# Summing the two halves of a gate weight in two TensorE products instead of in VectorE's addition, in every second batch of a gate table

## The reference, cut to what matters

```
s = einsum('bthpd,phnd->bthpn', q, sub_keys)          # 8 heads, 2 sides, 128 keys
sv, si = top_k(s, 16)                                 # per side
cand = sv[..., 0, :, None] + sv[..., 1, None, :]      # 16 x 16 candidates a head
cv, ci = top_k(cand, 16)
e1, e2 = the two key numbers of each of the 16        # expert = e1 * 128 + e2
gate = softmax(cv)
act = gelu(einsum('td,ted->te', hh, u_tab[ii]))
out = einsum('te,ted->td', gg * act, v_tab[ii])
x = x + out
```

## Time and profile before

| | us |
|---|---|
| median of three runs | 2497.33 |
| lowest and highest | 2496.42 and 2497.46 |
| profiled execution, its own time | 2494.71 |
| its span (first to last instruction) | 2492.9 |
| TensorE busy with products | 2435.0 (98%) |
| TensorE weight loads | 2278.8 (91%) |
| VectorE busy | 1666.5 (67%) |
| ScalarE busy | 1307.7 (52%) |
| GpSimd busy | 1126.6 (45%) |

### The profile page before, as it was taken

One profiled execution on the slowest core, in us unless ns is written; L12 is line 12 of the kernel. 1 busy time (PEld: TensorE's weight loads), 2 busy tenths in 40 slices (PEclk: granted clock), 3 DMA queues, 4 the chain that ended last, 5 costly groups with the idle time before them and its releaser, 6 DMA issues.

```text
span 2492.9 us, 46157 instructions
## 1 busy us (share of the span) xinstructions
PE 2435.0 (98%) x17096; PEld 2278.8 (91%) x17096; DVE 1666.5 (67%) x3053; ACT 1307.7 (52%) x2000; POOL 1126.6 (45%) x452
## 2 busy tenths in 40 slices
PE   9999999999999999999999999999999999999998
PEld 7999998999999998888799999999999999988886
DVE  7455713799997555777673666237999975567775
ACT  5565545555555444555555655555555554445554
POOL 4865776798674000000067767667976730000000
PEclk9999999999999999999999999999999999999999
DMA  6543554455667666777654335444557676667773
GB/s 225 169 135 113 168 186 135 148 175 174 247 238 253 223 206 223 243 243 244 207 180 157 133 127 169 163 150 152 184 181 248 239 257 205 216 227 236 237 243 132
DMA packets 186555, 485.59 MB, mean 195 GB/s; under 512 B 14400, under 2 KB 80960, under 8 KB 181824
## 3 DMA queue, kind: packets, MB, share of 16 engines
q1 hardware_dynamic: 179808, 442.74, 53.5%
q10 hardware_dynamic: 6624, 41.16, 4.8%
HBM read 449.24 MB, written 34.60 MB: 194 GB/s over the span
## 4 chain that ended last, share of the span: by engine, by line
PE 86%; DVE 6%; ACT 3%; POOL 2%; DMA 1%; issue 1%; SPq 0%; DVEq 0%; ACTq 0%; POOLq 0%
PE banks L800 28%; PE banks L464 17%; PE banks L466 16%; PE banks L465 16%; PE banks L776 2%; POOL w_lo L394 2%; PE banks L621 1%; ACT w_hi L832 1%; DVE arena L1596 1%; PE banks L720 1%; PE banks L704 1%; PE banks L685 1%; DVE arena L1439 1%; DMA o_f<-gates_dram 0%; DVE arena L1529 0%
## 5 line engine op out<-in xcount | busy, mean ns | idle before, releaser
L394 POOL TENSOR_TENSOR w_lo<-ring,w_hi 128x1024 fp32r<-128x1024 f32 x448 | 1126.4, 2526 | 899.2 <-ACT w_hi L832 898.7
L832 ACT ACTIVATE w_hi<-ring 128x1024 fp32r<-128x1024 f32 x776 | 816.9, 1056 | 406.0 <-PE banks L800 331.4
L464 PE MATMUL banks<-h_r,w_hi 128*128 128x256 f32 x3216 | 915.9, 285 | 2.7 <-DVE h_r L1364 1.8
L466 PE MATMUL banks<-h_r,w_lo 128*128 128x256 f32 x3216 | 911.2, 283 | 0.0
L465 PE MATMUL banks<-h_r,w_hi 128*128 128x256 f32 x3216 | 911.2, 283 | 0.0
L464 PEld LDWEIGHTS banks<-h_r,w_hi 128*128 128x128 f32 x3216 | 617.8, 192 | 7.9 <-issue 2.6
L465 PEld LDWEIGHTS banks<-h_r,w_hi 128*128 128x128 f32 x3216 | 617.9, 192 | 3.0 <-issue 0.5
L466 PEld LDWEIGHTS banks<-h_r,w_lo 128*128 128x128 f32 x3216 | 617.8, 192 | 0.0
L800 PE MATMUL banks<-w_hi,o_r 128*128 128x512 f32 x2048 | 559.2, 390 | 1.2 <-DVE o_r L1796 1.2
L800 PEld LDWEIGHTS banks<-w_hi,o_r 128*128 128x128 f32 x2048 | 380.3, 188 | 77.4 <-DVE o_r L1796 1.6
L1764 DVE TENSOR_TENSOR w_lo<-ring,w_hi 128x1024 fp32r<-128x1024 f32 x320 | 389.6, 1218 | 10.0 <-ACT w_hi L832 10.0
(11 more groups left out here) (268 smaller groups left out, 2609.9 us busy)
## 6 DMA issues: line engine op xcount, KB each, us to landing
ring<-in_stream SPq DMA_DIRECT2D x776, 512.0 KB, 3.3
gates_dram<-o_f ACTq DMA_DIRECT2D x32, 1024.0 KB, 5.5
o_f<-gates_dram SPq DMA_DIRECT2D x32, 1024.0 KB, 7.0
arena<-in_mem ACTq DMA_DIRECT2D x2, 1024.0 KB, 12.2
arena<-in_keys ACTq DMA_DIRECT2D x2, 1024.0 KB, 4.7
arena<-in_c_decay ACTq DMA_DIRECT2D x2, 768.0 KB, 5.3
x<-in_x SPq DMA_DIRECT2D x4, 256.0 KB, 5.8
out_dram<-arena SPq DMA_DIRECT2D x4, 256.0 KB, 2.3
```

What stands on the lines that cost most here:

```text
L394: pool.tensor_tensor(w_lo[:, s, :], ring[:, s, :], w_hi[:, s, :], ALU.subtract).then_inc(sem(f"low{s}"), 1)
L464: pe.matmul(out, lhs[0], rhs[0], start=first, stop=False)
L466: return pe.matmul(out, lhs[1], rhs[0], start=False, stop=last)
L832: act.activation(w_hi[:, s, :], ring[:, s, :], ACT.Copy).then_inc(sem(f"high{s}"), 1)
```

## The change

In batches of odd parity the four products of 256 columns become eight of 128 columns: for each token the high half and then the low half of `one2`, with the same `one1` as the stationary operand, into the same 128 columns of PSUM. The second of the two accumulates onto the first. ScalarE's copy (L1180) is unchanged and reads the first 128 columns of each token, which now hold the sum. VectorE's `spread_out` in these batches no longer adds: after the same wait for `table_high` it copies one column of PSUM to a scratch column and raises `spread_free`. Even batches are as before.

```diff
                     for t in range(BATCH):
-                        m = pe.matmul(table_out(parity)[:, t, :, :], one1[:, parity, t, :], one2[:, parity, t, :, :],
-                                      start=True, stop=True)
+                        if parity:
+                            for u in range(2):
+                                m = pe.matmul(table_out(parity)[:, t, 0, :], one1[:, parity, t, :], one2[:, parity, t, u, :],
+                                              start=(u == 0), stop=(u == 1))
+                        else:
+                            m = pe.matmul(table_out(parity)[:, t, :, :], one1[:, parity, t, :], one2[:, parity, t, :, :],
+                                          start=True, stop=True)
                     m.then_inc(sem("spread"), 1)
...
                     dve.wait_ge(sem("table_high"), l * BATCHES + i * (BATCHES // MIXED) + j + 1)
+                    if parity:
+                        dve.tensor_copy(mx[:, 0:1], bank[:, 0, 0:1]).then_inc(sem("spread_free"), 1)
+                        return
```

## The result

The changed kernel takes 2526.7 us (median of 4 runs, 2525.86 to 2529.03) against 2497.07 us for the kernel before on the same chip (4 runs, 2496.42 to 2497.46). The ratio is 1.012, 95% interval 1.0104 to 1.0136. The forecast was 2525.5 us, 28 us slower; it is 29.6 us slower.

A forecast was written before the change was run, and what follows sets the result against it. The prediction took TensorE to bound the woven stage: 2494.71 us profiled plus 28.2 for narrow products is 2522.9, plus 2.6 for the median gives 2525.5 us; own range 2518 to 2532, 8-in-10 range 2518 to 2590.

The forecast's parts named there:

- TensorE bounds the stage, VectorE is close behind: Woven stage: TensorE's own work sets the 3.36 us between batches; VectorE waits for it 17 times, 8.7 us in all.
- rival 3: Woven stage: VectorE was the hidden bound, so lightening it gives about 2470 us plus the products' cost; chance next to nothing.
- VectorE's edit is worth nothing: Odd batches, woven stage: VectorE gets some 26 to 37 us lighter, priced at zero because TensorE's work covers it.
- The load sets the pace of a narrow product: Odd batches: eight products at 0.115 us each, 0.44 us more a batch, 28.2 us in all; chance 0.52.
- The first and second rival: Odd batches: the first has narrow products at float32 rate, 2576 to 2595 us, chance 0.30; the second is rival 2.
- rival 2: Odd batches: weight loads partly or wholly hidden under the narrow products, 2495 to 2518 us; chance 0.15.
- The end of the stage moves with TensorE: Woven stage's end: gelu, two DMAs and TensorE's 0.61 us wait shift along, idle time stays, down stage does not move.
- The sum: Whole kernel: profiled 2494.71 us plus 28.2 makes 2522.9; plus 2.6 for the median of runs, 2525.5 us.

The follow-up runs named there:

- The early write: Changed kernel, but ScalarE issues the write of a half's last chunk of gates ahead of that step's gelu, not behind it: 2522.89 us, ratio 1.011.

## Why the prediction was right, step by step

**TensorE bounds the stage, VectorE is close behind.** Right. The run with VectorE's part alone moved nothing, and rival 3 had its test there. The view that told it beforehand was the table of waits and not the busy shares, in which both engines looked full.

**VectorE's edit is worth nothing.** Right, with 64 x (0.678 - 0.151) = 34 us taken from it (its busy time fell by 30.5), inside the 26 to 37 that were worked out.

**The load sets the pace of a narrow product.** Right, and the one step on which everything hung. The gap of 0.11 us between the first and the second load after idle time was the evidence; 0.115 us was taken, 0.112 measured. An odd batch costs 3.773 - 3.353 = 0.420 us more by the medians of the starts, where 0.44 was forecast, so 26.9 us in place of 28.2. The difference is the pace alone, 8 x 0.003 = 0.024 us a batch. The first product of an odd batch does give way to the second after 0.061 us, as its load is hidden under the 256-column product ahead of it, but the same time comes back at the end: the up product at L464 starts at 709.85 and L465 0.17 us later, since a load of 128 columns no longer fits under the last narrow product. From 709.00 to 710.02 makes 1.02 us, which is 8 x 0.112 + 0.12. The first and second rival fell with the same number, and the runs with 64 moving and 64 stationary columns showed that it is the load and not the width of the product. The sustained figure of 81 ns at 128 columns, from the Trainium skill, "TensorE: Matmul & The Clock Gate", section "Back-to-back issue gap", held for neither type here: 112 ns in fp32r, 56 in bf16. The 2508 us that the prediction works out from it lie in the range of rival 2, loads partly hidden, and not in that of rival 3, to which it refers them.

**The end of the stage moves with TensorE.** This step was wrong, and small. It said that the gelu, the two DMAs and the 0.61 us of idle time all move with TensorE, and that the down stage should not move. The gelu does move with it, but the write took 1.0 us longer and the read back 0.2, the wait grew to 1.8 us, and in the profiled execution the clock fell behind it: 2.5 us of waits and 3.1 us of half clock in two layers. The early write removed nearly all of both. What lengthens the write is not settled. Over all 32 writes its median is 6.5 us in the four kernels with the longer odd step (changed kernel, TensorE's part alone, 64 moving columns, early write in the changed kernel) and 5.5 us in the others with the usual step, so it goes with the length of the step. That the last write meets the refill of the weight ring at another moment is only argued: in the changed kernel the refill is issued as GpSimd ends, at about 805.0, and the write at 805.46, where before both went out within 0.02 us.

**The sum.** 26.9 of the 29.6 us between the medians are the pace of the narrow products. The remaining 2.7 are less than the 5.6 us that the end of the stage costs in the profiled execution. That execution took 2.3 us more than the median of the changed kernel, and the profiled one of before 2.4 us less than its median, so the two profiles are not the typical pair; half-clock stretches differ in length between executions, and the run with 64 moving columns showed the longer wait with such a stretch behind it in one layer only. How often it comes was not measured. That the forecast of 28.2 us came within 1.5 us of the 29.6 is in part luck: it took 1.3 us too much for the pace and nothing for the end of the stage.

## What to carry to other kernels

In these runs a product cost the longer of two things, streaming its moving columns and loading its stationary ones. In fp32r with 128 stationary columns the load needs 0.11 us, nearly as much as the 0.12 of a product of 256 moving columns, so splitting such a product in two nearly doubles its price (0.224 us for 0.120) though not one column is added. A load hides under one product only, so a narrow product also exposes the load of whatever comes behind it. Work that is taken from an engine which waits, and put on the one it waits for, is paid in full: look at who waits for whom in that stage before trading between two engines that both look busy. And when a stage changes its step, look again at the hand-over behind it, since a wait of TensorE that grew by a microsecond was followed by a stretch at half clock in five cases of six.

## What the runs showed of the hardware

- An fp32r load sets a pace of 0.112 us for 128 stationary columns and of no more than 0.061 for 64, with the product's moving columns at 128 in both; with 64 moving columns and 128 stationary it stays 0.112.
- The same 128 x 128 products in bf16 stand 0.056 us apart. Products of 256 columns stand 0.109 us apart in bf16 and 0.118 to 0.120 in fp32r.
- An fp32r load of 128 columns behind a product of about 0.06 us is not all hidden: counted from the first product of the batch, the second product behind it starts after 0.650 us for eight narrow products of 64 stationary columns in fp32r and after 0.632 for eight in bf16, and after 0.596 for an even batch.
- Accumulating a product onto the columns that the one ahead has just written costs nothing: 0.112 us with and without.
- An idle TensorE of 1.8 us ahead of the down stage was followed by 3.4 us at the 1.2 GHz level, and one of 0.6 us was not, nor any of up to 0.8 us. Of six such long waits (two layers in each of the changed kernel, TensorE's part alone and 64 moving columns) five were followed by it; in the second layer of the run with 64 moving columns the clock stayed up.
- VectorE's copy of one column out of PSUM takes 0.151 us, where a reciprocal of eight columns takes 0.20.
